# Feed-forward tails that close the first token tile before the second

## The reference

```python
def swiglu(u, wg, wu, wd):                       # first block, ffn0 to ffn3
    return (jax.nn.silu(u @ wg) * (u @ wu)) @ wd
h = h + 0.5 * swiglu(rmsnorm(h, g), wg, wu, wd)

f = swiglu_2(rms_norm(h, g[0]), w_in, w_out)     # second block, ffn4 to ffn7
h = h + FFN_RES * rms_norm(f, g[1])              # the product is normed again
hn = rms_norm(h, g[2])
m = even_mixer(hn, ...)                          # hyb; in the other layer odd_mixer, gla
h = h + rms_norm(m, g[3])
```

## Time and profile before

| | |
|---|---|
| median of 3 runs | 1913.53 us |
| the profiled execution, its span | 1912.22 us, 1910.3 us |
| PE busy | 1881.6 us (98%) |
| DVE busy | 1227.8 us (64%) |
| ACT busy | 944.5 us (49%) |
| POOL busy | 65.2 us (3%) |
| mean DMA rate | 177 GB/s |

### The profile page before, as it was taken

One profiled execution on the slowest core, in us unless ns is written; L12 is line 12 of the kernel. 1 busy time (PEld: TensorE's weight loads), 2 busy tenths in 40 slices (PEclk: granted clock), 3 DMA queues, 4 the chain that ended last, 5 costly groups with the idle time before them and its releaser, 6 DMA issues.

```text
span 1910.3 us, 34345 instructions
## 1 busy us (share of the span) xinstructions
PE 1881.6 (98%) x13542; PEld 1751.6 (92%) x13542; DVE 1227.8 (64%) x1646; ACT 944.5 (49%) x1296; POOL 65.2 (3%) x98
## 2 busy tenths in 40 slices
PE   9999999999999999999999999999999999999998
PEld 8999999999998888999999998899999998889997
DVE  6666766665555646666766689666676665877665
ACT  5444544454446635444544458554454446455443
POOL 0000100000001000000100000100010001010000
PEclk9999999999999999999999999999999999999999
DMA  7555355545553145455555343555545553344552
GB/s 285 198 198 198 140 198 198 187 174 202 184 196 125 67 143 199 191 193 197 199 198 196 145 144 104 207 229 187 184 169 200 195 198 122 133 145 176 196 198 99
DMA packets 61361, 338.83 MB, mean 177 GB/s; under 512 B 6960, under 2 KB 7344, under 8 KB 32880
## 3 DMA queue, kind: packets, MB, share of 16 engines
q1 hardware_dynamic: 59328, 330.00, 46.7%
q0 software_dynamic: 1968, 7.93, 1.3%
HBM read 336.85 MB, written 1.05 MB: 177 GB/s over the span
## 4 chain that ended last, share of the span: by engine, by line
PE 90%; DVE 4%; ACT 3%; issue 1%; DMA 1%; POOL 1%; SPq 0%; DVEq 0%; ACTq 0%; POOLq 0%
PE X L1620 54%; PE Y L1620 35%; ACT hiA L569 1%; DMA rawA<-in_wa 1%; DVE loA L1074 1%; DVE xl L1106 1%; DVE h L1149 0%; DVE xs L1142 0%; DVE arena L1408 0%; PE X L1660 0%; PE Y L2081 0%; PE X L1638 0%; POOL rstd L457 0%; PE X L1662 0%; ACT xh L615 0%
## 5 line engine op out<-in xcount | busy, mean ns | idle before, releaser
L1620 PE MATMUL X<-xh,hiA 128*128 128x256 f32 x2496 | 688.6, 277 | 2.8 <-DVE loA L1074 1.4
L1620 PE MATMUL X<-xl,hiA 128*128 128x256 f32 x2496 | 686.4, 277 | 0.0
L1074 DVE TENSOR_TENSOR loA<-rawA,hiA 128x2048 fp32r<-128x2048 f32 x219 | 501.6, 2291 | 275.2 <-ACT hiA L569 274.8
L1620 PE MATMUL X<-xh,loA 128*128 128x256 f32 x2496 | 677.7, 277 | 0.0
L1620 PEld LDWEIGHTS X<-xh,hiA 128*128 128x128 f32 x2496 | 468.6, 188 | 4.8 <-DVE loA L1074 1.6
L1620 PEld LDWEIGHTS X<-xl,hiA 128*128 128x128 f32 x2496 | 469.4, 188 | 0.0
L1620 PEld LDWEIGHTS X<-xh,loA 128*128 128x128 f32 x2496 | 463.3, 188 | 0.0
L569 ACT ACTIVATE hiA<-rawA 128x2048 fp32r<-128x2048 f32 (+1 forms) x235 | 423.6, 1803 | 55.5 <-PE Y L1620 30.6
L1620 PE MATMUL Y<-hiB,act_hl 128*128 128x512 f32 (+1 forms) x880 | 275.8, 346 | 0.0
L1620 PE MATMUL Y<-hiB,act_hh 128*128 128x512 f32 x704 | 275.3, 391 | 0.1
L1620 PE MATMUL Y<-loB,act_hh 128*128 128x512 f32 x704 | 275.0, 391 | 0.0
(11 more groups left out here) (253 smaller groups left out, 2184.8 us busy)
## 6 DMA issues: line engine op xcount, KB each, us to landing
rawA<-in_wa SPq DMA_DIRECT2D x221, 1024.0 KB, 5.4
rawB<-in_wb SPq DMA_DIRECT2D x181, 512.0 KB, 3.5
row_gain<-in_rows POOLq DMA_DIRECT2D x8, 512.0 KB, 4.5
arena<-in_gla POOLq DMA_DIRECT2D x1, 1280.0 KB, 8.7
h<-in_x SPq DMA_DIRECT2D x2, 512.0 KB, 4.1
out<-h SPq DMA_DIRECT2D x2, 512.0 KB, 2.7
arena<-in_pool POOLq DMA_DIRECT2D x1, 768.0 KB, 5.9
arena<-in_taps POOLq DMA_DIRECT2D x1, 576.0 KB, 4.5
```

Of the source, the lines that this page charges most:

```text
L1074: nc.vector.tensor_tensor(loA[p][:, :], rawA[p][:, :], hiA[p][:, :].bitcast(f32), ALU.subtract).then_inc(a_lo, 1)
L1620: return say(nc.tensor.matmul(*args, **kw))
```

## The change

```diff
@@ stage_plan
-        crossed = bool(before) and before["second"]
+        crossed = False
         early = raw and bool(before) and not crossed and before["kind"] in ("ffn", "mla")
@@ update (DVE, second block)
                 weighted(0, 0)
                 weighted(0, 1)
                 add(0, 0)
-                if s is plan[-1]:
-                    add(0, 1)
+                add(0, 1)
                 weighted(1, 0)
                 weighted(1, 1)
                 add(1, 0)
-                if s is not plan[-1]:
-                    add(0, 1)
                 add(1, 1)
@@ ffn (PE, the tail of all eight)
                 for half in range(2):
                     down_half(0, 0, half)
-                down_half(0, 1, 0)
                 pe.wait_ge(b_lo, b + NF)
+                pe.wait_ge(prod_hi, e + NF)
+                pb = (b + 1) % 2
+                for half in range(2):
+                    sl = HALF[half]
+                    mm(y_half(0, half), act_hh[:, 1, 0:P], hiB[pb][:, sl], start=False, stop=False)
+                    mm(y_half(0, half), act_hh[:, 1, 0:P], loB[pb][:, sl], start=False, stop=False)
                 pe.wait_ge(prod_lo, e + NF)
                 for half in range(2):
-                    down_half(1, 0, half, last=True).then_inc(y_part, 1)
+                    mm(y_half(0, half), act_hl[:, 1, 0:P], hiB[pb][:, HALF[half]], start=False, stop=True
+                       ).then_inc(y_part, 1)
+                down_half(0, 1, 0)
                 down_half(1, 1, 0, last=True).then_inc(y_part, 1)
                 down_half(0, 1, 1).then_inc(b_free, 1)
                 following(s)
```

## The result

| | before | changed |
|---|---|---|
| median, us | 1913.43 (15 runs, 1912.83 to 1915.02) | 1918.18 (15 runs, 1915.99 to 1920.48) |
| profiled execution, its span, us | 1912.22, 1910.3 | 1920.07, 1918.3 |

The ratio is 1.0026, with a 95% interval of 1.0018 to 1.0033: 4.75 us slower, just over the 0.2% that can be told from no change. The forecast of 1917.0 had the sign, and the range held the time; but "within 0.2%" had been given a little more (50%) than "slower" (46%), which it came to be. It isn't right in all its parts, as the seams show.

A forecast was written before the change was run, and what follows sets the result against it. PE's matmuls set the time, so only seams between stages could move. The terms +0.66 - 1.24 - 0.14 - 0.36 + 2.19 + 2.38 gave +3.5 us, a median of 1917.0, range 1914.8 to 1920.2.

The forecast's parts named there:

- tail, three seams: At ffn1 to kv, ffn0 to pool and ffn3 to final, the new tail's 0.22 us passes through whole: +0.66.
- hyb: At ffn4 to hyb, tile 0's second add moves ahead, so its diagonal is written when DVE comes free: -1.24 us.
- hyb to ffn5: Before ffn5, the new order of adds gains 0.36 us, but a late weight tile leaves only -0.14.
- gla to ffn7: Before ffn7, tile 0's transposes and seven idle ones go ahead in PE's wait: -0.36 us.
- ffn5 to ffn6: Early seam: the last down half comes behind tile 0's transposes and delays the relay by 3.29 us, partly given back: +2.19.
- ffn6 to gla: Early seam: the transpose moves by 3.29 us, and the first product waits for ACT's copies: +2.38.
- Rival A: The late down half replaces idle turns, so the two early seams cost nothing: -1.1 us, 1912.4; 7%.
- Rival B: Gains at hyb, ffn5 and ffn7 are taken back by ACT and DVE copies: +5.2 us, 1918.8; 13%.
- rival C: The clock falls in the early seams, each costing 5.4 us more: 1922.4 for one, 1927.8 for both; 6%.
- PE's wait for line 1149 in all: Sign in the changed trace: PE's total wait for this add goes from 3.6 to 7 us or more.
- Part 2: The order of adds at hyb, ffn5 and ffn7: -1.24, -0.14 and -0.36 us.
- PEclk under 9 in any slice: Sign that would show the forecast wrong: the page's PE clock figure falling under 9 in any slice.

The follow-up runs named there:

- experiment 4: Changed kernel with 25 idle transposes instead of 5 ahead of tile 1's at ffn6 and gla: 1915.51 us, ratio 1.0013.
- experiment 3: Kernel before with the new tail alone, in all eight stages, old flags and order of adds: 1914.95 us, ratio 1.0011.
- experiment 1: Changed kernel without the early transposes at ffn5 to ffn6 and ffn6 to gla: 1911.20 us, ratio 0.9989.
- experiment 7: Kernel before without its 20 idle transposes at each of ffn5, ffn6, gla and ffn7: 1915.32 us, ratio 1.0014.
- experiment 8: Kernel before with only the new order of adds and transposes, without the 20 idle transposes at each of four seams: 1911.58 us, ratio 0.9997.
- experiment 2: Kernel before with only the order of adds and transposes new, old tail, no early seam added: 1909.79 us, ratio 0.9981.
- experiment 6: Changed kernel with 15 idle transposes instead of 5 ahead of tile 1's at ffn6 and gla: 1915.93 us, ratio 1.0018.

## Why the prediction was right, and where it was wrong

| term | forecast | measured |
|---|---|---|
| tail, three seams | +0.66 | +0.25 + 0.22 + 0.18 = +0.65 |
| tail, mla and end | 0 | -0.01, -0.13 |
| hyb | -1.24 | -1.45 |
| hyb to ffn5 | -0.14 | -0.39 |
| gla to ffn7 | -0.36 | -0.29 (experiment 4, no fall) |
| ffn5 to ffn6 | +2.19 | +2.03 (experiment 4), +2.70 with a fall |
| ffn6 to gla | +2.38 | +2.31 |
| sum | +3.5 | +2.7 |
| the clock's falls, by difference | 0 | +2.0 (4.75 less 2.7) to +2.4 (against experiment 4) |

**The tail** was right in its steps: `act_hh` ends at 1394.74, PE's seventh matmul starts 0.14 behind it at 1394.88, 0.53 behind the sixth, and the eighth is 0.31 behind the seventh: 0.30 and 0.08 late, 0.38 in all. It was also right that only three seams pay, but experiment 3 shows that this hangs on the new order of adds. In the old one three more pay.

**The early seams** were right in place, mechanism and size. The relay kept its 3.09 us, PE's second pause was forecast from about 1401.3 to 1403.5 in the trace's old time, 2.2 us, and is 2.14; the first was given 0.6 and is 0.44. From the tail's first matmul to the product 13.1 us was forecast; it is 12.91 with the clock held and 13.58 with a fall. Rival A, that the reserve pays, is refuted by experiments 1 and 4: the filled seams stay long, the seams with the last down half in its old place are short.

**Hyb** was under-sized by 0.2. The step took DVE's row to end at the same time in both orders. It ends sooner, since the new row has no wait for the power in it: from tile 1's weighting to its first add 1.20 us (1097.57 to 1098.77) where it took 1.38 (1093.61 to 1094.99). From the first add to the diagonal it is now 3.86 us (1096.24 to 1100.10), and was 5.30 (1092.94 to 1098.24). Rival B, that the gains don't arrive, fell with it.

**Hyb to ffn5** was also under-sized. The late weight tile does take something back: the wait of the earlier trace rows is 1.54 us in the changed kernel and was 1.35. I had it take back 0.22 of a seam gain of 0.36; it takes 0.19 of 0.58.

**The step that failed is the clock's.** The forecast's own case had none, and rival C, with 6%, priced a fall at 5.4 us. Falls came in most runs, if the two upper groups (11 of 15) are taken for the runs with falls at the early seams, of which one was traced. One fall costs 1.1 to 1.5: against experiment 4, which held the clock, the fall at ffn6 adds 0.67 to the seam and 0.84 to the stage behind it (176.41 and 175.57), the one at gla 1.11 to gla's stretch (309.35 and 308.24). The one in the mla stage adds 1.16 there. So C was given far too small a chance and about four times the price. Two inferences led there. From 1.76 us of pause at hyb with the clock at 1.00 I took a safe length; experiment 7 shows a fall behind nothing longer than 1.53, experiment 8 one behind 1.09. And I let the clock stay low over as much work as a whole tail, with no row for it; it was low for 3.41 us at a time. The Trainium skill (TensorE: Matmul & The Clock Gate, What's actually happening) says that the gate goes back to half rate when PE has been idle. The traces agree in part: the falls at the early seams came behind pauses of 2.14 us, while 1.76 at hyb had none. With those pauses forecast at 2.2 us, the falls belonged in the sum, or at least among the likely cases.

So the total came out 1.2 us low as the difference of two errors: the seams 0.8 too dear, the clock 2.0 short. That it lies so near the forecast is in part luck. The clock's 2.0 is what the seams leave over, not a measured sum; in the profiled execution it closes: the seams' 2.7, the falls' 3.8 (0.67, 0.84, 1.11 and 1.16) and the start's 1.36 make 7.9 of the 8.0 us. The median of the changed kernel lies on the middle group of its runs; its fastest, at 1915.99, is near where the seams alone would put it (1913.43 + 2.7 = 1916.1).

Two of my own signs failed. PE's wait for line 1149 in all was to reach 7 us and reached 5.2, because the waits ahead of ffn5 and ffn7 vanish (0.85 at ffn7), which the same forecast's Part 2 implied. And "PEclk under 9 in any slice" could not have shown a fall that lasts 3.4 us in a slice of 48.

Left open: what sets whether the clock falls in a given execution. In the mla stage PE's two pauses ahead of the fall are 1.27 and 0.55 us in the changed kernel and 1.26 and 0.54 in the kernel before and in experiment 1; the changed kernel's execution and experiment 1's show a fall there, that of the kernel before doesn't. Whether the new tail makes that fall likelier was not tested.

## What to carry to other kernels

Work that starts a relay through several engines goes ahead of work that only fills PE, however idle the filler's slot seems: moving one 0.7 us down half behind eight transposes, which wait for adds themselves, delayed it by 3.2 us, and two thirds of that reached the next stage's first product. Judge a reordering on each list by itself; here three edits that were made together were worth -3.4 (order of adds and transposes), +1.4 (tail, experiment 1 less 2, of which the seams show 0.65 and falls of the clock may be the rest) and +6.7 (early transposes, falls included). Where a wait must stay, fill it with matmuls whose result nobody reads, and look for the clock in windows of a few microseconds rather than in the page's slices.

## What the runs showed of the hardware that was not expected

- Idle transposes of a constant hold the granted clock: with 25 or 15 of them in the pause the stretch stayed at 1.00 (experiments 4 and 6), with 5 it went to 0.66. Taking out the 20 of each seam cost 2.6 us in the kernel before and 2.2 in that of experiment 2, with the seams to ffn6 and gla of the same length.
- A fall isn't tied to one long pause: one came behind pauses of 0.62 and 1.53 us (experiment 7), none behind the 1.76 at hyb. Nor is it fixed by a seam's pauses: in experiment 8 the pair of 0.76 and 1.09 us ahead of ffn5 had a fall, and the pair of 0.75 and 1.09 ahead of ffn7 none.
- Each of the changed kernel's three falls lasted 3.41 us and cost 1.1 to 1.5, and the mean clock of single runs (0.996 to 0.999 in the changed kernel) shows that their number differs between executions. Their times lie in groups about 2 us apart. The spread of a kernel's runs, beside the mean granted clock of each, is a hint of a marginal pause before any trace is read.
